# The samples' vectors through DRAM: from the sync engine's queue to ScalarE's

## What is computed

```
proj = (xn @ P['w_in'][l]).astype(jnp.float32)
...
gates = jax.nn.sigmoid(proj[..., o4:]).reshape(B, T, N_MIX, D_MODEL)
ys = jnp.stack([y_a, y_b, y_c, y_d], axis=2)
branch = jnp.einsum('btmw,mwd->btmd', ys, P['w_branch'][l].astype(jnp.float32))
merged = jnp.sum(gates * branch, axis=2).astype(x.dtype)
```

```
sa = jnp.einsum('bhvk,bhk->bhv', S, -kk_t)
S = (S * w_t[:, :, None, :]
     + jnp.einsum('bhv,bhk->bhvk', sa, kk_t * a_t)
     + jnp.einsum('bhv,bhk->bhvk', v_t, k_t))
return S, jnp.einsum('bhvk,bhk->bhv', S, r_t)
```

## Time and profile before

| what | value |
|---|---|
| median of 3 runs | 2337.16 us |
| the runs | 2330.8, 2337.9, 2337.16 us |
| the profiled execution, its own time | 2338.85 us |
| its span, first to last instruction | 2336.7 us |
| mean granted TensorE clock | 0.926 of full speed |
| busy: PE | 1938.4 us (83%) |
| busy: DVE | 1424.4 us (61%) |
| busy: POOL | 635.2 us (27%) |
| busy: ACT | 583.2 us (25%) |
| DMA | 665.75 MB, 285 GB/s on average |

### The profile page before, as it was taken

The page is one execution under the profiler, slowest core; times in us unless marked ns, Lnnn a source line. Parts: engine busy times, 40 slices in busy tenths (PEclk is TensorE's granted clock), DMA queues, the critical chain, the costliest instruction groups (busy, mean ns, idle before and its releaser), DMA issues.

```text
span 2336.7 us, 25037 instructions
## 1 busy us (share of the span) xinstructions
PE 1938.4 (83%) x7668; PEld 1149.0 (49%) x7668; DVE 1424.4 (61%) x3607; ACT 583.2 (25%) x1552; POOL 635.2 (27%) x658
## 2 busy tenths in 40 slices
PE   6999889986887877778799888899777878787876
PEld 5777678752332333332378776787433333232323
DVE  1435464468877677785533343655687786877755
ACT  1211222033222232222221203210333222322222
POOL 0400000033444444434212000000444444344441
PEclk9999899998999898989989998999989889899899
DMA  6320133479999999999753210443999999999995
GB/s 257 112 107 2 76 138 130 159 294 412 404 421 422 411 422 414 415 412 412 308 205 119 80 57 25 167 142 113 375 399 422 422 421 415 420 409 414 412 422 232
DMA packets 102050, 665.75 MB, mean 285 GB/s; under 512 B 19984, under 2 KB 21936, under 8 KB 21936
## 3 DMA queue, kind: packets, MB, share of 16 engines
q0 software_dynamic: 76032, 553.68, 57.5%
q1 hardware_dynamic: 24208, 107.35, 12.8%
q10 hardware_dynamic: 1696, 3.39, 0.4%
HBM read 657.80 MB, written 6.58 MB: 284 GB/s over the span
## 4 chain that ended last, share of the span: by engine, by line
PE 51%; DMA 25%; DVE 14%; issue 6%; ACT 3%; POOL 1%; another core or an unknown queue 1%; DVEq 0%; POOLq 0%; SPq 0%; ACTq 0%
DMA arena<-in_uv,arena 24%; PE ps L890 18%; PE ps L504 9%; PE ps L566 7%; PE ps L854 3%; PE ps L823 2%; PE ps L837 2%; DVE ring L1718 1%; PE ps L484 1%; ACT arena L1166 1%; POOL arena L1234 1%; PE ps L514 1%; DVE arena L1648 1%; DVE arena L1641 1%
## 5 line engine op out<-in xcount | busy, mean ns | idle before, releaser
L890 PE MATMUL ps<-ring,arena 128*128 128x512 f32 x1056 | 563.1, 687 | 234.7 <-ACT arena L1166 234.4
L890 PE MATMUL ps<-arena 128*128 128x512 f32 x1056 | 488.9, 603 | 51.2 <-ACT arena L1166 50.5
L890 PEld LDWEIGHTS ps<-ring,arena 128*128 128x128 f32 x1056 | 223.5, 221 | 568.0 <-ACT arena L1166 338.7
L1718 DVE SCALAR_TENSOR_TENSOR arena<-arena 128x1024 f32<-128x1024 f32 x264 | 323.5, 1225 | 223.9 <-DMA arena<-in_uv,arena 222.8
L1234 POOL DMA_INDIRECT ring<-in_uv,arena x264 | 291.2, 1103 | 471.0 <-PE ps L890 429.7
L1718 DVE SCALAR_TENSOR_TENSOR ring<-ring,arena 128x1024 f32<-128x1024 f32 x264 | 322.8, 1223 | 124.6 <-DMA ring<-in_uv,arena 85.5
L890 PEld LDWEIGHTS ps<-arena 128*128 128x128 f32 x1056 | 191.6, 189 | 341.3 <-issue 195.5
L1234 POOL DMA_INDIRECT arena<-in_uv,arena x264 | 272.8, 1033 | 252.6 <-PE ps L890 202.8
L1164 ACT ACTIVATE arena<-arena 128x1 f32<-128x1 f32 x528 | 107.1, 203 | 913.4 <-DVE ring L1718 488.8
L566 PE MATMUL ps<-xn,ring 128*128 128x264 f32 x1024 | 243.5, 396 | 15.5 <-remote 13.5
L504 PE MATMUL ps<-xn,ring 128*128 128x264 f32 x1024 | 237.5, 392 | 6.0 <-DVE xn L1267 6.0
(11 more groups left out here) (394 smaller groups left out, 1674.2 us busy)
## 6 DMA issues: line engine op xcount, KB each, us to landing
ring<-in_w SPq DMA_DIRECT2D x88, 1024.0 KB, 4.9
ring<-in_uv,arena POOLq DMA_INDIRECT x264
arena<-in_uv,arena POOLq DMA_INDIRECT x264
st<-in_st SPq DMA_DIRECT2D x2, 2048.0 KB
out_st<-st SPq DMA_DIRECT2D x2, 2048.0 KB
const<-in_const ACTq DMA_DIRECT2D x1, 2665.0 KB, 11.4
arena<-in_keys SPq DMA_DIRECT2D x2, 1024.0 KB, 6.8
x<-in_x SPq DMA_DIRECT2D x1, 1056.0 KB, 5.0
```

The lines of the kernel that those rows point to most:

```text
L890: m = mm(bank(2 * tt + half, 512), dg[:, k, :], row(k)[:, D + 512 * half:D + 512 * half + 512], start=False, stop=False, skip_group_check= ...
L1718: stt(u, u, 1.0, xtok[:, tt, :], ALU.mult, ALU.mult, accum_out=hid[:, k:k + 1]).then_inc(S("dve_hid"), 1)
```

## The change

The seven DMAs and the wait between them leave SP's program and go into ScalarE's: the wait for the copies and the two writes behind the copy of `svt2`, the wait for the writes and the five reads behind the two Silu calls. Semaphores, sizes and layouts are the same. SP goes from block 23 straight to the shift output and block 24.

```diff
@@ SP, after block 23 of the layer @@
-                e.wait_ge(S("act_step"), step("act_svt"))
-                e.dma_start(O["scratch"][0:NGLA * NS, :], svt[0:NGLA * NS, :, :].rearrange("p a b -> p (a b)")).then_inc(S("sp_svw"), 16)
-                e.dma_start(O["scratch"][NGLA * NS:NVEC * NS, :], svt2[0:(NVEC - NGLA) * NS, :, :].rearrange("p a b -> p (a b)")).then_inc(S("sp_svw"), 16)
-                e.wait_ge(S("sp_svw"), 32)
-                e.dma_start(gv[:, :, :], O["scratch"].rearrange("(v b) (q k) -> (b q) v k", v=NVEC, k=16)).then_inc(S("sp_svr"), 16)
-                for n, v in enumerate((V_V, V_V + 1, V_V + 2, RW_V)):
-                    src = O["scratch"][v * NS:(v + 1) * NS, :].rearrange("b (h c) -> (b h) c", c=HD)
-                    e.dma_start(gvv[:, n, :], bc(src, 1, [32, 4, HD])).then_inc(S("sp_svr"), 16)
@@ ScalarE, after the copies of svt and svt2 @@
+                e.wait_ge(S("act_step"), step("act_svt"))
+                e.dma_start(O["scratch"][0:NGLA * NS, :], svt[0:NGLA * NS, :, :].rearrange("p a b -> p (a b)")).then_inc(S("sp_svw"), 16)
+                e.dma_start(O["scratch"][NGLA * NS:NVEC * NS, :], svt2[0:(NVEC - NGLA) * NS, :, :].rearrange("p a b -> p (a b)")).then_inc(S("sp_svw"), 16)
                 act(proj[:, HG + 6:HG + 8, :], proj[:, HG + 6:HG + 8, :], ACT.Silu)
                 act(proj[:, RT + 6:RT + 8, :], proj[:, RT + 6:RT + 8, :], ACT.Silu)
+                e.wait_ge(S("sp_svw"), 32)
+                e.dma_start(gv[:, :, :], O["scratch"].rearrange("(v b) (q k) -> (b q) v k", v=NVEC, k=16)).then_inc(S("sp_svr"), 16)
+                for n, v in enumerate((V_V, V_V + 1, V_V + 2, RW_V)):
+                    src = O["scratch"][v * NS:(v + 1) * NS, :].rearrange("b (h c) -> (b h) c", c=HD)
+                    e.dma_start(gvv[:, n, :], bc(src, 1, [32, 4, HD])).then_inc(S("sp_svr"), 16)
                 act(proj[:, HG:HG + 6, :], proj[:, HG:HG + 6, :], ACT.Sigmoid)
```

## The result

The changed kernel takes 2342.28 us (median of 16 runs, 2336.81 to 2351.57) against 2336.19 for the one before (16 runs). The ratio is 1.0029 with a 95% interval of 1.0018 to 1.0040: **slower by 0.3%, about 7 us**, where no difference was forecast. One of the 16 runs before, 2758.95 us, was a slow one and stays out of the ratio. The profiled execution took 2346.76 us with a span of 2344.9.

What follows compares the result with a forecast made beforehand. VectorE's chain was taken to bound the stage up to L794, TensorE the rest. Layer 1 at 0.0 and layer 2 at -0.1 us summed to -0.1, against the median 2337.16: 2337.1 us, range 2331.5 to 2341.5.

Steps and rivals of the forecast that it cites:

- the 7 us of TensorE's pause: TensorE's standstill before gate tile 16; only 0.49 and 0.96 us of its lateness were said to reach VectorE.
- the weight block was the bound: Rival: with block 24 early, all of TensorE's pause and slow clock before tile 16 comes back, 19 us, 2318; chance 0.04.
- The Silus hidden: On ScalarE, the two Silu calls run within the writes' time and don't delay the read issues.
- the read issues at SP's durations: ScalarE was to issue the five reads as SP did, 0.39 us and then 3.33 us with gaps.
- Quick reads: Rival: ScalarE issues each read in 0.4 us; VectorE gains 1.5 and 1.8 us, 2333.8; chance 0.12.
- the issues hold ScalarE: Rival: each issue holds ScalarE 1.4 us; 3.9 us longer in layer 1, 4.1 in layer 2, 2345.1; chance 0.07.
- The writes' landing: Samples' writes beside block 26 land 0.45 us later, bounds 0 and +1.0; over 4.5 us to land would show it wrong.
- if they share fairly: Block 26 and the writes split the DMA engines, so the writes' 0.6 us of work takes twice that: +0.45 us.
- all of the block's data first: Upper bound of the writes' delay: block 26's data moves wholly ahead of the writes, +1.0 us.
- The row of glob: Example for the upper bound: 6 KB landed 5.3 us after issue beside the load of x, where out_p_n took 2.9 alone.
- All stages behind are bounded by what follows L794, which doesn't move: After TensorE's product L794, later stages were to keep their times, so no further term was added.
- the crowded write: Rival: the writes beside block 26 cost +1.0 us or a little more per layer, 2338 to 2340; chance 0.1.

Runs made afterwards that it cites:

- run 4: The kernel before, all DMAs on SP, with only blocks 24 and 25 issued ahead of the samples' writes; 2344.73 us, ratio 1.0026.
- the second profile: The changed kernel run and profiled once more with nothing altered; ratio to the kernel before 1.0029.
- run 1: The changed kernel with block 26 held back by SP until both writes have landed, blocks 24 and 25 still early; ratio to the kernel before 1.0003.
- run 6: The changed kernel with two of the last six gate tiles moved ahead of L794 (7 tiles there, not 5); ratio to the kernel before 1.0008.

## Why the prediction was wrong, step by step

- **That the 7 us of TensorE's pause would not come back:** right. The pause stayed ahead of tile 16 (8.60 and 8.68), now released by ScalarE's copy of tile 14, as named. The rival "the weight block was the bound" (2318) is refuted twice, by the changed kernel and by run 4.
- **The Silus hidden, the read issues at SP's durations:** right. Reads are issued in 3.88 us against 3.76. "Quick reads" and "the issues hold ScalarE" both fall: one issue in four is long (up to 1.49 us), as on SP.
- **The writes' landing, taken as +0.45 us with a bound of +1.0:** this is the term that failed. The reads left 1.99 us later in layer 1 and 2.56 in layer 2, beyond the bound, and the second write took 5.0 and 5.3 us to land, past the 4.5 that the prediction named as a sign of being wrong. The place of block 26 was nearly right: with this execution's shift of 0.7 us it was to be issued at 299.9 with its data over at 304.1, and it was issued at 299.75 with its last row over at 304.71. What failed is "if they share fairly". They don't: 120 of the block's 128 rows had started when the writes' first row did, 1.67 us later than without the block, and the last row ended 1.99 later. That is the mechanism of the prediction's own upper bound, "all of the block's data first", but the bound was too small. The prediction shows no working for +1.0; alone, the writes' first row starts 0.84 us after their issue, at 303.1, and behind a block that is over at 304.8 it comes 1.7 us later. The instruction packet and the nine rows behind it were no term of the sum. The row of glob that was set aside as far (5.3 us beside a load, 2.9 alone) had the right size, +2.4; no run shows whether for the same reason.
- **What followed from it:** the mechanism was worked out rightly. With +1.99 in the place of +0.45 the same sum gives +1.5 in layer 1 and, with 2.85 us of later start less the 0.96 of vanished waiting, +1.9 in layer 2; measured at L794 are +1.56 and +2.01.
- **"All stages behind are bounded by what follows L794, which doesn't move":** wrong. L794 moved, and in layer 2 the clock fell behind it for another 1.7 us. The sum has no price for a low clock behind L794, though the fall ahead of tile 16 was in its rows.
- **The range:** 2341.5 as its upper end took the crowded write at +1.0 a layer or a little more, and 2 us for the spread of medians. The stages' 1.6 + 3.7 = 5.3 us, and 2.1 + 3.9 = 6.0 in the second profile, lie outside it, and the medians' 6 to 7 us with them. The remaining 1 us is not attributed. Two side sums are loose without bearing on this: by the layers' own steps a delay of 0 gives -1.0, not -0.8, and in the rival of the slow issues TensorE's side has 0.1 us of margin and not 0.5, so that it would come out 0.3 to 0.5 us longer in each layer.
- The Trainium skill, in DMA: Bandwidth & Descriptors, section Issuing engines are not separate DMA queues, says that DMAs of all issuing engines run on the same 16 DMA engines and interleave. The traces agree that the queue makes no difference: the writes were as late from ScalarE's queue (5.39 to 6.06 us) as from SP's behind the block (5.40, 6.18). Interleaving shows in run 1, where the reads' rows run among the block's, and hardly with the writes, which start when 109 to 123 of the block's 128 rows have started in all the profiles with the block ahead of them.

Left open is why the clock falls behind L785 in layer 2 of the changed kernel and not in layer 1, nor in run 1, whose pauses there are as long (1.79 and 1.58 us). It did so in both profiles. In run 6, with a pause of 8.95 us ahead of tile 16 and none ahead of L785, it did not, so the long pause alone doesn't bring it. No run separates the causes further. Also open is why nearly all of the block's rows go ahead of the writes' while the reads' rows go among them.

## What to carry to other kernels

A DMA leg of a few us on the critical path has to be checked for what else the queues will then send, not only for which queue sends it: freeing SP let a 1 MB load go 1.8 us ahead of two small writes and cost them 2 to 3 us, whichever engine issued them. Look at the packets of the transfer one waits for, when its first and its last row move, before pricing what a neighbour does to it: the mean share of the DMA engines doesn't show who goes first. Time that an engine waits is only worth something where its next wait has been filled: with the two blocks sent early and nothing else the pause moved on to a worse place and cost 6 us through the clock, and with two tiles moved as well the kernel gained 13 us.

## What was not expected of the hardware

- Two small writes issued 1.8 to 2.1 us behind a 1 MB load had their first row start 2.5 to 3.0 us after their issue in place of 0.8 to 0.9, with 109 to 123 of the load's 128 rows started, from either queue. The second write landed 5.0 to 5.8 us after its issue in place of 2.7 to 3.2. With the load sent 0.2 us behind the first read, VectorE's start came 7.0 to 7.2 us after that read's issue in place of 5.0 to 5.4.
- The last nine of the writes' 144 rows started within 0.02 us of the end of a 16 KB instruction packet in 16 of 20 stages, up to 1 us behind the other 135, and the reads left 1.3 us after that packet's end.
- A pause of TensorE of 1.41 us was followed, 2.3 us after TensorE had started again, by a stretch at 1.2 GHz from about 1508 to 1511, and pauses of 1.58 and 1.79 us in another kernel were not.
- Moving one pause of 7 us by 28 us within the stage, with VectorE's chain unchanged, cost 1.9 and 3.6 us in the two layers.
